# Reordering the second block of a two-block transformer kernel: three PSUM banks for projections, turnings between them

## What is computed

```python
for l in range(2):
    hn = rms_norm_2(h, attn_norm_g[l])
    proj = hn @ w_in[l]                   # 1024 x 4096, cut into 12 pieces
    a_o = moba_attention(...)             # 6 heads, causal softmax
    b_o = diff_attention(...)             # 4 heads, softmax1 - lam * softmax2, then a norm per head
    c_o = stick_breaking_attention(...)   # 6 heads: abs, exp, log, running sums, exp
    h = h + concat(a_o*silu(mg), b_o*silu(dg), c_o*silu(sg)) @ w_out[l]
    q = rms_norm_2(h, xattn_norm_g[l]) @ w_xq[l]
    h = h + softmax(q k^T) v @ w_xo[l]    # cross attention, 4 heads, on a memory of 256 rows
out = rms_norm_2(h, final_norm_g)
```

## Time and profile before

| what | value |
|---|---|
| median of 3 runs | 2230.76 us (2230.68 to 2236.69) |
| profiled execution, span | 2226.2 us |
| median less that span | 4.6 us |
| second block: first and last PE instruction | 1769.42 and 2218.5 us |
| PE busy over the span | 1947.9 us (87%) |
| DVE, ACT busy over the span | 782.9 us (35%), 433.4 us (19%) |

### The profile page before, as it was taken

How to read it: one execution, slowest core, us unless ns; L and a number is a source line. 1 busy time by engine, 2 the same in 40 slices (tenths; PEclk the granted TensorE clock), 3 DMA queues, 4 the chain that set the end, 5 groups by cost and what they waited for, 6 DMA issues and landing times.

```text
span 2226.2 us, 29861 instructions
## 1 busy us (share of the span) xinstructions
PE 1947.9 (87%) x12745; PEld 1074.3 (48%) x12745; DVE 782.9 (35%) x1742; ACT 433.4 (19%) x1095; POOL 26.9 (1%) x52
## 2 busy tenths in 40 slices
PE   6999999999988888889999875677776699999997
PEld 4444544455444433335778531233342347664765
DVE  2587865344122121241374402100110235433543
ACT  2122711022111111021341111000000222222222
POOL 3000000000000000000000000000000000000000
PEclk9999999999999999999999988889888999999999
DMA  9644235416999999992327499999999833233320
GB/s 297 224 165 148 107 114 212 166 59 256 406 421 423 423 423 423 422 403 95 134 105 291 181 380 424 422 416 415 417 416 420 353 113 114 96 132 114 114 85 19
DMA packets 133826, 575.91 MB, mean 259 GB/s; under 512 B 7448, under 2 KB 16128, under 8 KB 92736
## 3 DMA queue, kind: packets, MB, share of 16 engines
q1 hardware_dynamic: 129312, 556.82, 62.9%
q0 software_dynamic: 3872, 17.00, 2.2%
q10 hardware_dynamic: 512, 0.19, 0.0%
HBM read 572.93 MB, written 1.05 MB: 258 GB/s over the span
## 4 chain that ended last, share of the span: by engine, by line
PE 69%; DMA 21%; DVE 5%; ACT 2%; issue 2%; SPq 0%; DVEq 0%; ACTq 0%
DMA ring<-w_up_e 16%; PE ps L854 10%; PE ps L1236 7%; PE ps L1202 6%; PE ps L1292 5%; PE ps L843 5%; PE ps L1016 4%; PE ps L870 4%; PE ps L1300 3%; DMA ring<-w_down_e 3%; PE ps L1434 2%; PE ps L1067 2%; DMA ring<-w_xkv 2%; PE ps L1168 2%; PE ps L1272 1%
## 5 line engine op out<-in xcount | busy, mean ns | idle before, releaser
L1202 PE MATMUL ps<-ring,reg_bc 128*32 128x512 f32 x2896 | 376.3, 661 | 147.2 <-DMA ring<-w_up_e 147.2
L1202 PEld LDWEIGHTS ps<-ring,reg_bc 128*32 128x32 f32 x2896 | 89.1, 116 | 409.6 <-DMA ring<-w_up_e 236.9
L854 PE MATMUL ps<-reg_a,ring 128*128 128x512 f32 (+1 forms) x768 | 253.7, 487 | 0.0
L2400 DVE TENSOR_TENSOR xall<-xall,ps 128x512 f32<-128x512 f32 x48 | 32.8, 687 | 452.8 <-PE ps L1168 452.8
L854 PEld LDWEIGHTS ps<-reg_a,ring 128*128 128x128 f32 x768 | 143.8, 190 | 96.4 <-issue 86.7
L2443 DVE TENSOR_TENSOR reg_a<-ps,reg_e 32x256 f32<-32x256 f32 x192 | 80.7, 420 | 192.2 <-PE ps L1236 189.8
L1292 PE MATMUL ps<-ring,reg_a 128*128 128x512 f32 (+2 forms) x448 | 140.8, 472 | 0.5 <-issue 0.2
L1775 ACT ACTIVATE reg_bc<-ps 128x512 f32<-128x512 f32 x47 | 28.1, 597 | 571.1 <-PE ps L1202 571.1
L1236 PE MATMUL ps<-ring,reg_bc 128*32 128x256 f32 x2048 | 116.5, 380 | 14.6 <-issue 12.4
L843 PE MATMUL ps<-ring,reg_a 128*128 128x512 f32 (+1 forms) x288 | 112.5, 545 | 0.4 <-DVE reg_a L2018 0.4
L1292 PEld LDWEIGHTS ps<-ring,reg_a 128*128 128x128 f32 x448 | 74.6, 191 | 60.5 <-issue 58.9
(11 more groups left out here) (378 smaller groups left out, 2302.9 us busy)
## 6 DMA issues: line engine op xcount, KB each, us to landing
ring<-w_down_e SPq DMA_DIRECT2D x64, 2048.0 KB, 15.6
ring<-w_gate_e SPq DMA_DIRECT2D x123, 1024.0 KB, 11.3
ring<-w_up_e SPq DMA_DIRECT2D x123, 1024.0 KB, 14.5
ring<-w_in SPq DMA_DIRECT2D x34, 2048.0 KB, 9.1
ring<-w_ada SPq DMA_DIRECT2D x24, 2048.0 KB, 11.2
ring<-w_out SPq DMA_DIRECT2D x8, 2048.0 KB, 8.4
ring<-w_xkv SPq DMA_DIRECT2D x8, 1024.0 KB, 15.5
ring<-w_br_global SPq DMA_DIRECT2D x4, 1024.0 KB, 7.8
```

Of the source, the lines that this page charges most:

```text
L854: mm = pe.matmul(ps[j][:, 0:n], w[:, k, j * P:(j + 1) * P], HT[:, k, 0:n], start=(k == 0), stop=(k == KC - 1))
L1202: mm = pe.matmul(ps[s][32 * j:32 * j + 32, :], XGT[l][:, e // 4, s, 2 * q + k, e % 4 * CAP:(e % 4 + 1) * CAP], w[j // 2][:, k, (j % 2) * C ...
```

## The change

Only the second block changes, and no arithmetic does.

- **Banks.** The groups from H0 to H5 rotate over banks 0, 1 and 5; the others keep 0 and 1. Bank 5 is free for that since `values(i)` now always writes bank 4, and waits for the read of the unit before it. The first use of bank 5 (H1) and `values(0)` wait until `exps(1)` has read the diff scores.
- **PE order.** After each small turning group a projection follows before the product that needs the turned tile: G01 behind QA, G10 behind QB, H1 behind QM0, H2 behind QM1, S0 behind QM2, S5 behind D0 and D1. D0 and D1 move from unit 7 to unit 5. `scores(1)` comes ahead of `turn(0)`. `values(6)` comes ahead of `turn(7)`, and `values(7)` goes into the middle of O00. `turn_tile` of the cross norm's tile 0 moves ahead of O11. `cross_turn(0)` goes into Q1 before its last quarter, `cross_turn(1)` into X10 after half of it; `cross_scores(1)` comes behind `cross_values(0)`.
- **Cross values of tile 1** use banks 5 (heads 0, 1) and 4 (heads 2, 3), are read in two halves, and the output group starts on the first half.
- **Between the layers** the turning of tile 0 for layer 1 moves ahead of the last half of `cross_out(1)`, and the 14 matmuls of `keep_warm` before G30 stay in layer 0 alone.
- **ACT and DVE** follow with their copies. On DVE `diff_gates` moves ahead of `maxima(0)`, `gate(1)` ahead of `scale_probs(2)`, `heads_out(8)` ahead of `maxima(9)`, and the additions of X00 and X10 ahead of `heads_out(9)`. On ACT D0 and D1 are copied behind `stick_logs(0)` and S2.

```diff
-    negmax=7, exps=7, sk_abs=3, sk_eabs=3, sk_log=3, sk_weights=3, lin_mm0=0, lin_mm1=0, lin_rd0=0, lin_rd1=0,
+    negmax=7, exps=7, sk_abs=3, sk_eabs=3, sk_log=3, sk_weights=3, cross_half=1, cross_half_read=1,
     rope_diff=2, rope_moba=2, gate_exp=6, diff_gate=2, diff_merged=1, xo_mm=2, xo_rd=2,
 )
 
 
-GROUPS = ("G30 G40 G31 G41 G00 QA QB G01 G10 G11 V20 V21 H0 QM0 QM1 QM2 H1 H2 S0 S1 S2 S3 S4 S5 "
-          "V60 V61 V70 V71 H3 D0 D1 H4 H5 O00 O10 O01 O11 Q0 Q1 X00 X10").split()
-BANK_OF = {name: (n % 2, n // 2 + 1) for n, name in enumerate(GROUPS)}
-for bank in range(2):
+GROUPS = [("G30 G40 G31 G41 G00 QA G01 QB G10 G11 V20 V21", (0, 1)),
+          ("H0 QM0 H1 QM1 H2 QM2 S0 S3 S1 S4 V60 S2 D0 D1 S5 V70 V61 V71 H3 H4 H5", (0, 1, 5)),
+          ("O00 O10 O01 O11 Q0 Q1 X00 X10", (0, 1))]
+BANK_OF = {}
+for names, banks in GROUPS:
+    for n, name in enumerate(names.split()):
+        b = banks[n % len(banks)]
+        BANK_OF[name] = (b, sum(other == b for other, _ in BANK_OF.values()) + 1)
+for bank in (0, 1, 5):
...
@@ -1278,7 +1287,9 @@
             def fill(name, mms):
 
                 bank, n = BANK_OF[name]
-                if l or n > 1:
+                if bank == 5 and n == 1:
+                    pe.wait_ge(*at(f"exps@{l}", 2))
+                elif l or n > 1:
...
@@ -1346,14 +1357,16 @@
 
             def values(i):
                 kind, u = UNITS[i]
-                for name in {"diff": ("G40", "G41"), "stick": ("V60", "V61", "V70", "V71"),
+                for name in {"diff": ("G40", "G41"), "stick": ("V70", "V71") if u == 2 else ("V60", "V61"),
                              "moba": ("G10", "G11", "V20", "V21")}[kind]:
                     pe.wait_ge(*read(name, l))
+                if i == 0:
+                    pe.wait_ge(*at(f"exps@{l}", 2))
                 pe.wait_ge(*at(f"unit_pt@{l}", i + 1))
-                if i >= 2:
-                    pe.wait_ge(*at(f"unit_read@{l}", i - 1))
+                if i:
+                    pe.wait_ge(*at(f"unit_read@{l}", i))
                 v0 = {"diff": 1664, "stick": 2176, "moba": 768}[kind] + P * u
-                o, pt = ps[4 + i % 2], PT2[i % 2].rearrange("p (h n) -> p h n", h=2)
+                o, pt = ps[4][:, 0:SEQ], PT2[i % 2].rearrange("p (h n) -> p h n", h=2)
                 for h in range(2):
                     v = [PROJ2[:, j, v0 + 64 * h:v0 + 64 * h + 64] for j in range(2)]
                     if kind == "diff":
...
@@ -1410,14 +1431,27 @@
                 i = where[("xo", l, 0)]
                 w = slab_view(i, 4, D)
                 slab_wait(pe, i)
-                pe.wait_ge(*at(f"unit_read@{l}", 9 + t))
+                if t == 0:
+                    pe.wait_ge(*at(f"unit_read@{l}", 9))
+                else:
+                    pe.wait_ge(*at(f"cross_half_read@{l}", 1))
                 for half in range(2):
                     if t == 0:
-                        fill(f"X{half}0", lambda b: [pe.matmul(ps[b][:, :], XOT[:, k, 0:P],
-                                                               w[:, k, half * COL:(half + 1) * COL],
-                                                               start=(k == 0), stop=(k == 3)) for k in range(4)])
+
+                        def mms(b):
+                            for k in range(4):
+                                if (half, k) == (1, 2):
+                                    cross_turn(1)
+                                yield pe.matmul(ps[b][:, :], XOT[:, k, 0:P], w[:, k, half * COL:(half + 1) * COL],
+                                                start=(k == 0), stop=(k == 3))
+                        fill(f"X{half}0", mms)
                     else:
                         for k in range(4):
+                            if (half, k) == (0, 2):
+                                pe.wait_ge(*at(f"unit_read@{l}", 10))
+                            if l == 0 and (half, k) == (1, 0):
+                                pe.wait_ge(*at("n3@1_xn", 1))
+                                turn_tile("n3@1", 0, XN2)
                             mm = pe.matmul(ps[2 + half][:, :], XOT[:, k, P:2 * P], w[:, k, half * COL:(half + 1) * COL],
                                            start=(k == 0), stop=(k == 3))
                         mm.then_inc(sem(f"xo_mm@{l}"), 1)
...
@@ -1429,6 +1463,8 @@
 
                 def mms(b):
                     for q, k in enumerate((3, 4, 0, 1, 2, 5, 6, 7)):
+                        if k == 5 and (n, t) == (0, 0):
+                            values(7)
                         if k >= 5 and (n, t) == (0, 0):
                             pe.wait_ge(*at(f"unit_read@{l}", k + 1))
                         yield pe.matmul(ps[b][:, :], OT2[:, k, t * P:t * P + P], w[:, k, :],
@@ -1437,9 +1473,9 @@
 
             if l == 0:
                 keep_warm(7, 45)
-            pe.wait_ge(*at(f"n3@{l}_xn", 1))
-            turn_tile(f"n3@{l}", 0, XN2)
-            keep_warm(7, 14)
+                pe.wait_ge(*at("n3@0_xn", 1))
+                turn_tile("n3@0", 0, XN2)
+                keep_warm(7, 14)
             tile_ready(f"n3@{l}", 0)
             rows("G30", "in2", 3, 0, HT2)
             pe.wait_ge(*at(f"n3@{l}_xn", 2))
@@ -1451,69 +1487,71 @@
             rows("G00", "in2", 0, 0, HT2)
             pe.wait_ge(*at(f"rope_diff@{l}", 2))
             turn_qk("QA", 1152, 1408)
+            rows("G01", "in2", 0, 1, HT2)
             scores(0)
             turn_qk("QB", 1280, 1536)
-            rows("G01", "in2", 0, 1, HT2)
+            rows("G10", "in2", 1, 0, HT2)
+            pe.wait_ge(*at(f"exps@{l}", 1))
+            scores(1)
             turn(0)
-            scores(1)
-            rows("G10", "in2", 1, 0, HT2)
+            rows("G11", "in2", 1, 1, HT2)
+            values(0)
+            rows("V20", "in2", 2, 0, HT2, 0, P)
             turn(1)
-            values(0)
-            rows("G11", "in2", 1, 1, HT2)
-            for t in range(2):
-                rows(f"V2{t}", "in2", 2, t, HT2, 0, P)
+            rows("V21", "in2", 2, 1, HT2, 0, P)
             values(1)
             columns("H0", "in2", 2, 1, HT2)
...
             turn(4)
             values(3)
             scores(5)
-            columns("S4", "in2", 6, 0, HT2)
+            columns("S2", "in2", 5, 2, HT2)
+            pe.wait_ge(*at(f"diff_merged@{l}", 1))
+            for u in range(2):
+                fill(f"D{u}", lambda b: [pe.transpose(ps[b][:, t * P:t * P + P], DO[:, t, P * u:P * u + P], ident[:, :])
+                                         for t in range(2)])
             columns("S5", "in2", 6, 1, HT2)
-            rows("V60", "in2", 6, 0, HT2, SEQ, COL)
+            rows("V70", "in2", 7, 0, HT2, 0, P)
...
             columns("H3", "in2", 7, 1, HT2)
             turn(6)
             values(5)
             scores(7)
-            pe.wait_ge(*at(f"diff_merged@{l}", 1))
-            for u in range(2):
-                fill(f"D{u}", lambda b: [pe.transpose(ps[b][:, t * P:t * P + P], DO[:, t, P * u:P * u + P], ident[:, :])
-                                         for t in range(2)])
             columns("H4", "in2", 7, 2, HT2)
             columns("H5", "in2", 7, 3, HT2)
+            values(6)
             turn(7)
-            values(6)
-            values(7)
             for u in range(2):
                 pe.wait_ge(*read(f"D{u}", l))
             out_rows(0, 0)
             out_rows(1, 0)
             out_rows(0, 1)
+            pe.wait_ge(*at(f"n4@{l}_xn", 1))
+            pe.wait_ge(*at(f"unit_read@{l}", 8))
+            pe.wait_ge(*read("H5", l))
+            turn_tile(f"n4@{l}", 0, XN4)
             out_rows(1, 1)
 
-            pe.wait_ge(*at(f"n4@{l}_xn", 1))
-            turn_tile(f"n4@{l}", 0, XN4)
...
@@ -1521,11 +1559,9 @@
             cross_scores(0)
             tile_ready(f"n4@{l}", 1)
             cross_queries(1)
-            cross_turn(0)
+            cross_values(0)
             cross_scores(1)
-            cross_values(0)
             cross_out(0)
-            cross_turn(1)
             cross_values(1)
             cross_out(1)
...
@@ -2726,15 +2768,17 @@
             gained(f"n4@{l}", 1, HT2, 32 + 8 * l)
             maxima(8)
             scale_probs(8)
+            heads_out(8)
             maxima(9)
-            heads_out(8)
             scale_probs(9)
-            heads_out(9)
             add_out("X00", 0, 0)
             add_out("X10", 1, 0)
+            heads_out(9)
             if l == 0:
                 normed("n3@1", 0, XN2)
             for half in range(2):
+                if l == 0 and half:
```

More of the change, by code:

```diff
@@ L401, in slab_freed @@
             return at(f"xo_mm@{l}", 2)
-        name = {"in2": ("G01", "G11", "H2", "G31", "G41", "S3", "V61", "H5"), "out2": ("O01", "O11"), "xq": ("Q1",)}[kind][s]
+        name = {"in2": ("G01", "G11", "H2", "G31", "G41", "S2", "V61", "H5"), "out2": ("O01", "O11"), "xq": ("Q1",)}[kind][s]
         bank, n = BANK_OF[name]
@@ L529, in width, with cross_bank @@
         return 4 if i < 2 or i >= 8 else 2
+    def cross_bank(t, h):
```

(55 more changed lines are left out.)

40 lines of the change are left out of this document (24 added, 16 removed).

## The result

The changed kernel takes 2206.57 us (median of 4 runs, 2204.35 to 2213.13) against 2230.72 (2228.91 to 2236.69): a ratio of 0.9896, 95% interval 0.9882 to 0.9909. Predicted were 2205.6 us in a range of 2202 to 2213. In two later comparisons the ratio was 0.9874 (0.9857 to 0.9890) and 0.9885 (0.9867 to 0.9903).

What follows compares the result with a forecast made beforehand. PE was taken to bound the second block, so only its waits or work could shorten it. The terms, 21.2 + 3.1 + 1.5 - 0.6 = 25.2 us, took the median from 2230.8 to 2205.6 us, range 2202 to 2213.

Steps and rivals of the forecast that it cites:

- Rivals 3 and 4: Second block: 3, DVE becomes the bound, 2260 us, chance 0.02; 4, waits were not PE's bound, 2230 us, chance 0.03.
- Term 1: PE's waits in both layers of the second block get a cover: 27.4 us less 6.2 remaining, 21.2 us saved.
- The largest ... goes: behind D1 now stand S5 and V70: Ahead of H4 in each layer: the 2.48 us wait goes, because other groups now follow D1.
- Term 2: H4 and H5, both layers: without the long wait ahead, the clock stays up and 3.1 us come back.
- rival 1: At Q0: the clock falls there instead and gives back 3.1 us, 2208.7 us; chance 0.12.
- A clock below 0.98 behind Q0: Second block, behind Q0: a sign that the prediction is wrong, since it expected clock 1.00 throughout.
- The price of nothing for Q0: At Q0's new 2.1 us wait: clock loss counted as nothing, with 3.1 us as the other end.
- Term 3: Between the layers: the 14 matmuls left out save 1.5 us.
- Term 4: Eight places a layer with covers within 0.5 us of the need: 0.6 us lost in all, 8 us at worst.
- Rival 2: The places with level covers are all late: 8 us back, 2213 us; chance 0.12.
- The step from span to median: Whole kernel: span falls from 2226.2 to 2201.0 us, and 4.6 us around it give the median of 2205.6.
- PE's start away from 1769.4: Start of the second block on PE: any other start time was named a sign that the prediction is wrong.

Runs made afterwards that it cites:

- experiment 3: Changed kernel with the turning of the cross norm's tile 0 back behind O11 on PE: block 421.6 us, 1.2 less than the changed kernel.
- experiment 2: Changed kernel with DVE's `gained` ahead of its addition of O11: block 418.5 us, 4.2 less than the changed kernel.
- experiment 9: Changed kernel with `turn(7)` ahead of `values(6)` again: block 426.0 us, against 422.8 for the changed kernel with a steady clock.
- experiment 10: Changed kernel with the cross values of tile 1 read once from one bank: block 425.0 us, 2.2 more than the changed kernel.
- Experiment 6: Changed kernel, three banks kept, D0 and D1 back in unit 7 ahead of H4: block 421.9 us, 0.8 less than the changed kernel.
- experiments 7 and 8: 7: kernel before, D0 and D1 alone moved to unit 5, block 451.6 us, 2.5 more; 8: changed kernel with two banks, block 458.0 us, 35 more.
- experiment 5: Kernel before with 20 unread matmuls filling the wait ahead of H4 in both layers: block 445.9 us, 3.1 less than before.

## Why the prediction was right

- **What bounds the kernel.** Right: with PE's waits gone the block shortened by their sum, while DVE and ACT kept their busy times. Rivals 3 and 4 fall.
- **Term 1, 21.2 us.** Right in size. The three remaining waits are where they were put: G01 0.34, QM2 0.32, Q0 1.86 recorded, for 0.3 to 0.6, 0.3 to 0.6 and 1.8 to 2.1. Start to start they cost 2 x (0.51 + 0.46 + 2.03) = 6.0 us, for 6.2. That the wait at Q0 grows although the turning moved ahead, by 0.6 to 0.7 us a layer, is shown by experiment 3, and its cause by experiment 2. The level cover of `turn(7)` is shown by experiment 9, the read in halves by experiment 10.
- **One cause in term 1 was put too simply.** "The largest ... goes: behind D1 now stand S5 and V70" gives it to the new place of D0 and D1. Experiment 6 shows that the third bank removes the wait without the new place. With two banks the new place does remove it too, but experiments 7 and 8 show longer waits in its stead, 3.29 us ahead of D1 and 3.58 ahead of O00. The sum didn't suffer, since the change has both.
- **Term 2, 3.1 us.** Right, shown by experiment 5 with 3.1. Its open end, rival 1 (the clock falls at Q0), came true in one of two layers of the first profile and in none of the next two profiles. "A clock below 0.98 behind Q0" was a sign of being wrong, and the first profile shows it, with 0.81.
- **The price of nothing for Q0 was luck.** I had taken one wait of 1.95 us with a steady clock as proof; it was one draw. Behind the same wait, which stands once in each layer of the first block, the clock fell in 18 of 28 places over all 14 traces (the last section has rows of one). The trace of before has both of its two steady. At Q0 itself it fell in 2 of 14, near the 0.12 that rival 1 had, but not for the reason given. The Trainium skill's page "TensorE: Matmul & The Clock Gate", section "Why this matters for your kernels", asks only that longer idle gaps than these be avoided; these traces disagree, with falls behind 1.86, 1.95, 2.48 and 2.70 us.
- **Term 3, 1.5 us,** was not tried by itself; the 14 matmuls are gone from PE's program there, and PE's list shows no wait for the norm between the layers.
- **Term 4, 0.6 us lost at level places.** Nothing measurable was: terms 1 to 3 make 25.8 us, and the block with a steady clock is 26.3 shorter. Rival 2 falls. In the first profile the clock's 1.6 us stands in its place, 24.6.
- **The step from span to median.** I added the 4.6 us between the median and the span of before. Only 1.8 us of that lies around a span, as the profile after shows; the other 2.8 are that the profiled execution of before had a short first block. The sum was made of differences, so the forecast didn't suffer, but "PE's start away from 1769.4", a sign of being wrong by the prediction, was met at 1779.06 and was no sign of anything. That the first median came within 1 us of the forecast is partly luck: the changed kernel's three medians go from 2204.2 to 2208.0.

## What to carry to other kernels

With hand-written orders, list each wait of the bounding engine, ask what independent work could stand in it, and follow the buffer as well as the data: here the order without the third bank was 9 us slower than before, and moving one pair of groups alone 2.5 us. When a producer is moved ahead, move its consumer on the other engines past whatever it queues behind: without that the turning ahead of O11 lost 1.2 us, and adding it brought 4.2. Where spans vary for reasons outside the change, compare the length of the changed stretch: it repeated to 0.01 us with a steady clock, while whole runs on one chip varied by 8.
